# MLP second products as one level of Strassen's scheme: seven quarter-block products in place of eight

## The reference, cut to what matters

```
hm = rms_norm(x, g_mlp)                                 # x: 512 x 1024
x = x + square(relu(hm @ w_up)) @ w_down                # w_up: 1024 x 4096, w_down: 4096 x 1024
return rms_norm(x, g_final)
```

## Time and profile before

| what | us |
|---|---|
| median of 3 runs (1577.17 to 1579.16) | 1579.07 |
| the profiled execution | 1579.46 |
| its span, first to last instruction | 1577.7 |
| PE busy in the span | 1531.7 (97%) |
| DVE / ACT / POOL busy | 890.2 / 715.3 / 223.5 |
| granted TensorE clock, mean | 0.991 |

### The profile page before, as it was taken

The page is one execution under the profiler, slowest core; times in us unless marked ns, Lnnn a source line. Parts: engine busy times, 40 slices in busy tenths (PEclk is TensorE's granted clock), DMA queues, the critical chain, the costliest instruction groups (busy, mean ns, idle before and its releaser), DMA issues.

```text
span 1577.7 us, 19176 instructions
## 1 busy us (share of the span) xinstructions
PE 1531.7 (97%) x7086; PEld 1239.6 (79%) x7086; DVE 890.2 (56%) x1753; ACT 715.3 (45%) x1630; POOL 223.5 (14%) x194
## 2 busy tenths in 40 slices
PE   7998999999999999999899999999999999999998
PEld 5886777877898777777587878788777888888886
DVE  6467485657565566666457557664455444434344
ACT  6553343334355667665335354442344433324243
POOL 3203020202120003122022005220001100000001
PEclk9999999999999999999999999999999999999999
DMA  6522121323424221112133312134323333333332
GB/s 194 161 68 80 54 80 55 107 68 120 119 76 147 77 61 56 54 56 67 41 121 94 94 55 67 56 109 131 93 81 94 94 93 96 105 94 93 97 103 81
DMA packets 88636, 141.56 MB, mean 90 GB/s; under 512 B 6368, under 2 KB 36448, under 8 KB 88544
## 3 DMA queue, kind: packets, MB, share of 16 engines
q1 hardware_dynamic: 87824, 139.55, 29.3%
q10 hardware_dynamic: 720, 0.80, 0.2%
HBM read 138.23 MB, written 2.10 MB: 89 GB/s over the span
## 4 chain that ended last, share of the span: by engine, by line
PE 79%; DVE 8%; ACT 5%; issue 3%; POOL 3%; DMA 2%; SPq 0%; ACTq 0%; POOLq 0%; DVEq 0%
PE banks L1259 12%; PE banks L1261 12%; PE banks L1260 12%; PE banks L1264 10%; PE banks L1266 10%; PE banks L1265 10%; PE banks L1222 3%; DVE sb_w_split L1964 3%; ACT sb_junk L1529 2%; DVE sb_arena L1973 2%; PE banks L1437 1%; PE banks L1384 1%; ACT sb_w_split L1561 1%; PE banks L1500 1%; DVE sb_arena L1964 1%
## 5 line engine op out<-in xcount | busy, mean ns | idle before, releaser
L1964 DVE TENSOR_TENSOR sb_w_split<-sb_raw,sb_w_split 128x512 fp32r<-128x512 f32 (+4 forms) x530 | 345.0, 693 | 365.9 <-ACT sb_w_split L1561 365.5
L1561 ACT ACTIVATE sb_w_split<-sb_raw 128x512 fp32r<-128x512 f32 (+4 forms) x530 | 288.1, 592 | 411.2 <-PE banks L1261 192.0
L1259 PE MATMUL banks<-sb_actA,sb_w_split 128*128 128x512 f32 x672 | 277.1, 412 | 2.8 <-DVE sb_arena L1964 2.5
L1261 PE MATMUL banks<-sb_actA,sb_w_split 128*128 128x512 f32 x672 | 263.0, 391 | 0.0
L1260 PE MATMUL banks<-sb_actA,sb_w_split 128*128 128x512 f32 x672 | 262.1, 390 | 0.0
L1264 PE MATMUL banks<-sb_w_split,sb_actB 128*128 128x512 f32 (+2 forms) x464 | 181.4, 391 | 1.6 <-DVE sb_w_split L1964 1.6
L1266 PE MATMUL banks<-sb_w_split,sb_actB 128*128 128x512 f32 (+2 forms) x464 | 175.9, 379 | 0.0
L1265 PE MATMUL banks<-sb_w_split,sb_actB 128*128 128x512 f32 (+2 forms) x464 | 175.5, 378 | 0.0
L1264 PE MATMUL banks<-sb_w_split,sb_actA 128*128 128x512 f32 (+1 forms) x384 | 154.4, 402 | 13.5 <-DVE sb_w_split L1964 9.6
L1259 PEld LDWEIGHTS banks<-sb_actA,sb_w_split 128*128 128x128 f32 x672 | 126.5, 188 | 32.7 <-issue 7.1
L1266 PE MATMUL banks<-sb_w_split,sb_actA 128*128 128x512 f32 (+1 forms) x384 | 150.3, 391 | 0.0
(11 more groups left out here) (226 smaller groups left out, 2188.2 us busy)
## 6 DMA issues: line engine op xcount, KB each, us to landing
sb_raw<-in_a_w_in SPq DMA_DIRECT2D x66, 256.0 KB, 3.0
sb_raw<-in_w_up SPq DMA_DIRECT2D x32, 512.0 KB, 3.8
sb_raw<-in_w_down SPq DMA_DIRECT2D x32, 512.0 KB, 3.8
sb_raw<-in_w_in SPq DMA_DIRECT2D x24, 512.0 KB, 3.7
sb_raw<-in_mem_w_kv SPq DMA_DIRECT2D x16, 512.0 KB, 3.8
sb_raw<-in_w_ckv SPq DMA_DIRECT2D x16, 512.0 KB, 3.8
sb_raw<-in_a_w_in SPq DMA_DIRECT2D x15, 512.0 KB, 3.7
sb_raw<-in_a_w_out SPq DMA_DIRECT2D x12, 512.0 KB, 3.9
```

The lines of the kernel that those rows point to most:

```text
L1259: pe.op.matmul(out, hi[:, cs], x.hi(k), start=i == 0, stop=False)
L1261: t = pe.op.matmul(out, lo[:, cs], x.hi(k), start=False, stop=last_i)
L1561: act.op.activation(hi[:, cs], raw[:, cs], ACT.Copy).then_inc(act.mark(m("w_hi"), 2 * n + part + 1), 1)
L1964: dve.op.tensor_tensor(out, a, b, op).then_inc(dve.mark(*mark) if mark else dve.tick(), 1)
```

## The change

**The product.** Let a block's hidden activations be cut into quarters F(rows, cols), rows being two halves of the 512 tokens and cols two halves of the 1024 hidden units, and its block of `w_down` into quarters w0 to w3 of 512 x 512. Eight quarter products are replaced by seven: P1 = F00·w0, P2 = F01·w2, Q5 = S1·T1, P6 = S2·T2, Q3 = S4·w3, Q7 = S3·T3, N4 = -F11·T4, with sums S of activation quarters and T of weight quarters. Each is 2 banks (256 tokens) x 4 k-tiles: 2 chunks of 12 matmuls. Their order is P1, P2, Q5, P6, Q3, Q7, N4.

**Weights.** The quarters are loaded whole (`fetchR`, 1 MB each; w0 and w1 into arena space, w2 and w3 into the space of `x_res`, for block 0 only after the last `xt`). POOL makes T1, T3, T2, T4 in place (`tsum`), 1024 columns an instruction, two per sum. The splits of these chunks are one instruction of 1024 columns on ACT and one on DVE, not two of 512.

**Activations.** `relu` now evicts with the row of 1/r (a step `nrow` e on PE and ACT replaces `esum`), ACT squares into a plain buffer, and for each product and k-pair a step `g` (ACT high part, DVE low part) or `gp` (ACT high part, POOL low part) writes the operands. The sums are `s1` (DVE) and `ssum` 2, 4, 3 (POOL).

**Landing.** A product is added into `x_tok` and/or a buffer `first_sum`: ten landings, each over two token tiles, so 20 DVE instructions of 512 columns per block in place of 8 evictions. In block 3 six more POOL additions (`fix`) take `first_sum` over.

```diff
-            add(f"up{b}{g}", ("w_up",), D_MODEL, [(b * D_MODEL + g * 512, 512)], "feature", "hE", "relu")
-        for half in range(2):
-            add(f"dn{b}{half}", ("w_down",), D_MODEL, [(half * 512, 512)], "token", f"f{b}", "tok", k0=b * D_MODEL)
+            add(f"up{b}{g}", ("w_up",), D_MODEL, [(b * D_MODEL + g * 256 + c, 256) for c in (0, 512)], "feature", "hE", "relu")
+        for i in range(7):
+            add(f"wn{b}{i}", None, 512, [(0, 512)], "token", f"F{b}{i}", "wn" if len(LANDS[i]) == 1 else "wn2",
+                tokens=SEQ // 2)
...
+LANDS = {P1: (("x", 0, 0, ALU.add), ("sum", 0, 0, ALU.subtract)), P2: (("x", 0, 0, ALU.add),),
+         Q5: (("x", 0, 1, ALU.add), ("x", 1, 1, ALU.add)), P6: (("sum", 0, 0, ALU.add),), Q3: (("x", 0, 1, ALU.add),),
+         Q7: (("x", 1, 1, ALU.add), ("x", 1, 0, ALU.subtract)), N4: (("x", 1, 0, ALU.subtract),)}
...
+        if b:
+            p.soon.extend([[("fetchR", b, 0)], [("fetchR", b, 1)], [("tsum", b, 1, 0)], [("fetchR", b, 3)],
+                           [("tsum", b, 1, 1)], [("fetchR", b, 2)], [("tsum", b, 3, 0)], [("tsum", b, 3, 1)]])
...
+        p.soon.extend([[("g", b, P1, 0)], [("g", b, P2, 0)], [("s1", b, 0), ("g", b, Q5, 0)], [("ssum", b, 2, 0)],
+                       [("gp", b, P6, 0)], [("ssum", b, 4, 0)], [("gp", b, Q3, 0)], [("ssum", b, 3, 0)]])
+        p.product(f"up{b}1", into=banks(4) if b else (0, 1, 2, 3),
+                  tail=lambda j: [("relu", b, up_tile(1, j))] + ([("g", b, P1, 1)] if j == 1 else []))
+        if b == 0:
+            p.need(("tsum", 0, 3, 1))
+        work = {P1: [[("g", b, P2, 1)], [("s1", b, 1), ("g", b, Q5, 1)], [("gp", b, Q7, 0)], [("ssum", b, 2, 1)]],
+                P2: [[("tsum", b, 2, 0)], [("gp", b, P6, 1)], [("g", b, N4, 0)], [("tsum", b, 2, 1)]],
+                Q5: [[("ssum", b, 4, 1)], [("gp", b, Q3, 1)], [("ssum", b, 3, 1)], [("gp", b, Q7, 1)]],
+                P6: [[("g", b, N4, 1)], [("tsum", b, 4, 0)], [("tsum", b, 4, 1)]],
+                Q3: [[("fix", n)] for n in range(3)] if b == 3 else [], Q7: [], N4: []}
+        for i in WINO_ORDER:
+            p.soon.extend(work[i])
...
+            p.product(f"wn{b}{i}", into=banks(2), tail=tail, whole=b == 3 and i == N4)
```

In the split of such a chunk (ACT, then DVE), and in the sums on POOL:

```diff
+                made = {Q5: 1, P6: 2, Q7: 3, N4: 4}.get(i)
+                if made:
+                    act.wait_ge(*m.at("t_sum", ("tsum", b, made, c)))
+                else:
+                    act.wait_ge(m(f"dma_quarter{WEIGHT[i]}"), 16 * (b + 1))
+                act.wait_ge(*m.chunk_done(n - SPLIT_SLOTS))
+                act.op.activation(hi, raw, ACT.Copy).then_inc(act.mark(m("w_hi"), 2 * n + 2), 2)
...
+            elif t == 2:
+                pool.wait_ge(*m.wino_split(b, Q5, c))
+                tensor(total, total, w[3], ALU.add, *m.at("t_sum", step))
```

More of the change, by code:

```diff
@@ L408, in need, with product @@
                 self.force(step)
-    def product(self, name, before_ev=(), soon=None, into=None, first=True, tail=None):
+    def product(self, name, before_ev=(), soon=None, into=None, first=True, tail=None, whole=False):
         pr = PRODUCTS[name]
@@ L415, in product @@
         ks, i, n_j = k_tiles(name), 0, n_out(name)
-        spans = [(c,) for c in range(len(pr.order))] if tail is None else [(0,), tuple(range(1, len(pr.order)))]
+        spans = [tuple(range(len(pr.order)))] if whole else [(c,) for c in range(len(pr.order))]
         for span in spans:
@@ L778, in order_of_work @@
     p.put(("load_g",))
-    p.side(0, [("sqp", "e", 7)], lag=0)
-    p.side(0, (), ("nsq", "e"), ("esum",), lag=4000)
+    scales(0, "e", after=[("sqp", "e", 7)])
     for j in range(TT):
@@ L783, in order_of_work @@
             p.side(0, (), ("xt", j, g))
-    for b in range(4):
[L785 to L789, removed]
+    for i in (0, 1):
+        p.put(("fetchR", 0, i))
+    for i in (3, 2):
+        p.side(0, (), ("fetchR", 0, i))
@@ new lines, in order_of_work, with banks @@
+    for t in (1, 3):
+        for c in range(2):
+            p.side(0, (), ("tsum", 0, t, c), lag=0)
+    bank = 4
+    def banks(n):
+        nonlocal bank
+        bank = (bank + n) % 8
+        return [(bank - n + i) % 8 for i in range(n)]
+    for b in range(4):
+        if b:
+            p.soon.extend([[("fetchR", b, 0)], [("fetchR", b, 1)], [("tsum", b, 1, 0)], [("fetchR", b, 3)],
+                           [("tsum", b, 1, 1)], [("fetchR", b, 2)], [("tsum", b, 3, 0)], [("tsum", b, 3, 1)]])
+        p.product(f"up{b}0", [("nrow", "e")], into=banks(4) if b else (0, 1, 2, 3),
+                  tail=lambda j: [("relu", b, up_tile(0, j))])
+        p.soon.extend([[("g", b, P1, 0)], [("g", b, P2, 0)], [("s1", b, 0), ("g", b, Q5, 0)], [("ssum", b, 2, 0)],
[11 more added lines that the diff above has]
+            p.soon.extend(work[i])
+            tail = None
+            if b == 3 and i in (P2, Q7):
+                tail = lambda j: [("fsq", int(i == Q7), 2 * (i == Q7) + j), ("fg", 2 * (i == Q7) + j)]
+            elif b == 3 and i in (Q3, N4):
+                tail = lambda j: [(kind, *([int(i == Q3)] if kind == "fsq" else []), 2 * (i == N4) + j)
+                                  for kind in ("fsq", "fin", "store")]
+            p.product(f"wn{b}{i}", into=banks(2), tail=tail, whole=b == 3 and i == N4)
@@ L1174, in raw_total, with wino_split @@
     def raw_total(self, n):
-        return 16 * sum(len(PRODUCTS[self.plan.chunks[m][0]].parts) for m in range(n % RAW_SLOTS, n + 1, RAW_SLOTS))
+        return 16 * sum(len(PRODUCTS[self.plan.chunks[m][0]].parts) for m in range(n % RAW_SLOTS, n + 1, RAW_SLOTS)
+                        if not is_wino(self.plan.chunks[m][0]))
+    def wino_split(self, b, i, c):
+        return self("w_lo"), 2 * self.plan.chunk_of[f"wn{b}{i}", c] + 2
 class Stream:
```

225 lines of the change are left out of this document (181 added, 44 removed).

## The result

| | before | after |
|---|---|---|
| median, us | 1578.12 (1575.03 to 1579.16, 4 runs) | 1630.23 (1628.19 to 1634.11, 4 runs) |
| span of the profiled execution, us | 1577.7 | 1626.1 |
| granted TensorE clock, mean | 0.991 | 0.983 |

The ratio is 1.0344, 95% interval 1.0324 to 1.0364. The direction was forecast, the size was not: 52 us slower where I had 18, and outside the range of 1562 to 1612.

A forecast was written before the change was run, and what follows sets the result against it. PE bounds the kernel, busy 97% of the span. -21.8 + 0.4 + 4 x 8 (lateness) + 4 (block 0) + 3.5 (block 3 and end) = +18.1 on 1579.5 gives 1597.6, median 1597; range 1562 to 1612.

The forecast's parts named there:

- block 0: In block 0, w2 and w3 load late, so P2's first chunk is 4 us late beyond the usual lateness; bounds 0 to 6.
- block 3 and the end: In block 3, `fg` costs 2.2 us, Q3's chains ahead of N4's splits about 1, the end 0.6: together 3.5, from 0.6 to 6.
- PE's part: Down products: 96 matmuls fewer save 21.8 us, `nrow` adds 0.4; a block's seven products take 38.1 us, not 43.5.
- the prices of ACT and DVE: Seven products: ACT 1.05 us a 1024-column split, 0.63 a conversion; DVE 1.15 to 1.22 a split, 0.60 a landing.
- what costs nothing: Blocks 1 to 3, up products: loading the quarters and making T1 and T3 there adds no time.
- POOL's prices: POOL's sums: 2.0 us for 1024 columns, 1.05 for 512, making 15.4 us of work in the first four products.
- The turns: Seven products: DVE's splits, `g` and `s1` wait while a POOL addition runs, landings don't; without this the sum is 1578.
- case 1: The forecast: DVE, held by POOL, makes the first four products late, 6 to 10 us a block: 1588 to 1608; chance 0.50.
- case 4: POOL becomes the bound, ACT behind it: 13 us a block or more, stretches above 50 us, 1618; chance 0.10.
- Case 2: The turns don't matter, POOL falls into DVE's landings: 3.1 us a block, 1578, from 1573 to 1587; chance 0.14.
- case 3: Split slots hide nearly all lateness, PE stays the bound: 0 to 1.5 us a block, 1564, 1559 to 1572; chance 0.26.
- The walk: One block's seven products followed chunk by chunk: lateness 10 us with turns, 3.1 without; 8 taken, for turns possibly won.

The follow-up runs named there:

- pool_few: Changed kernel with GpSimd's weight sums, activation sums and low parts worked on 16 columns only, results left out: 1578.16 us, ratio 1.0008.
- pool_fill: Changed kernel with each of GpSimd's sums and low parts replaced by two memsets of its output, which read nothing from SBUF: 1585.06 us, ratio 1.0054.
- t4_late: Changed kernel with the two halves of weight sum T4 moved from P6's steps to Q3's in the list: 1623.84 us, ratio 1.029.
- late_fin: Changed kernel with block 3's `fg` of tiles 0 and 1 moved after Q3, their norm chains and stores after Q7's evictions: 1621.56 us, ratio 1.0285.
- close_on_vector: Kernel of on_vector's moves in the order just in time, with block 3's six repairs on VectorE too, the first one place later: 1589.2 us, ratio 1.0073.
- on_vector: Changed kernel with the sums and low parts that GpSimd makes inside the seven products moved to VectorE, same order: 1612.75 us, ratio 1.0224.
- the order just in time: on_vector's moves against the changed kernel, with sums placed near their use, copies of x earlier, block 3's closing work behind Q3 and Q7: 1590.31 us, ratio 1.0081.

## Why the prediction fell short

By the starts of the matmuls in the two profiled executions (before: stretches of 43.52 each):

| term | forecast | measured |
|---|---|---|
| 96 matmuls fewer | -21.8 | -21.8 |
| `nrow` | +0.4 | +0.5 |
| blocks 1 and 2 | 2 x 8 | 2 x 13.35 |
| block 0 | 8 + 4 | 18.4 |
| block 3 and the end | 8 + 3.5 | 26.2 + 0.3 |
| start of the up products (1218.1, 1216.2) | 0 | -2.0 |
| sum | +18.1 | +48.3, of 48.4 between the spans (rounding) |

Of the 30.2 us between the two sums, 21.4 are the four blocks' 13.35 for 8, 9.7 are block 3 and the end beyond that (13.2 for 3.5), 1.0 is block 0 (5.0 for 4) and 0.1 `nrow`; the start takes 2.0 off. Two terms failed, then: the lateness of a block, and the end. The row of the start is not the change's: in the profiled executions of all kernels the up products begin between 1211.6 and 1218.5.

**PE's part, the prices of ACT and DVE, and what costs nothing** held: splits 1.22 and landings 0.68 listed, ACT's 1.05, up products 43.52 with all quarters loaded and T1 and T3 made in them. POOL's prices did not hold: where nothing holds it, it lists 2.40 us for 1024 columns and 1.28 for 512, where I had 2.0 and 1.05, so its work in the four products was 18.6 us and not 15.4. Two slips of the working weigh little: DVE has six small instructions and not five (31.7 us, not 31), and 2 MB are four loads of 512 KB, not three, so block 0's low bound was taken for a shorter transfer.

**The turns** are shown by pool_few and pool_fill: the mechanism of case 1, and of case 4 (below). Case 2 is out (landings free, yet 13.35 us), and so is case 3.

**The walk** named the right chunks: 1.0, 0.8, 2.8, 1.3, 1.2 and 2.9 us late, measured 1.2, 0.6, 0.8 + 2.1, 1.5, 1.4 and 3.3. Its 10 became 10.9. The step that failed is the one after it: "a turn won there is worth 1 us; I take 8". No turn was won. The lateness is a sum of waits in series, and I had discounted its largest terms for luck. With 2.9 us a block that is some 12 of the 21.4 us. Most of the other 2.45 a block is the clock.

**The clock** was missing from the sum. PE in block 1, around a gap, and the granted clock of the two slow spells:

```profile
1386.35 0.47 PE L1370 MATMUL banks<-sb_w_split,sb_actB 128*128 128x512 f32 x1 [1.97 <-issue]
...
1387.58 0.43 PE L1372 MATMUL banks<-sb_w_split,sb_actB 128*128 128x512 f32 x1
1387.82 0.63 PE L1370 MATMUL banks<-sb_w_split,sb_actB 128*128 128x512 f32 x1
1388.24 0.63 PE L1371 MATMUL banks<-sb_w_split,sb_actB 128*128 128x512 f32 x1
```

```profile
1387.80:1391.20 3.40, 3.33 (x8) 2.15 (x7) 2.09 (x3) 1.21 (x2) 3.06 (x2) 0.50 0.00 0
1401.00:1404.40 3.40, 3.38 (x9) 2.67 (x10) 3.40 (x5) 0.00 (x0) 0.00 (x0) 0.57 0.02 5
```

The starts of matmuls are 0.43 us apart there, not 0.227: the lower level, 1.2 GHz. It came after idle times of 2.1 and 3.3 us and lasted some 3.4 us each time. In the MLP of the kernel before no matmul is so spaced. What it costs is less than what it slows: block 2, with the same gaps, has the second spell alone (8 starts 0.43 apart against 13) and the same 51.45 us. The first spell only fills time in which PE waits in block 2: the fifth and sixth gaps are 1.9 us together in block 1, and 2.8 in block 2. And t4_late has the same seven gaps in both blocks, but in its block 1 no such spell at all. Its blocks 1 and 2:

```profile
1363.67:1413.56 49.89, 40.10 (x170) 30.98 (x168) 41.15 (x43) 20.16 (x27) 25.80 (x13) 1.00 0.08 25
1457.08:1508.57 51.49, 41.67 (x169) 32.13 (x168) 41.40 (x43) 20.16 (x27) 25.83 (x13) 0.97 0.08 25
```

So the clock is worth 1.6 us of a steady block's 13.35. The rest of the 2.45 is mostly the second start after a gap, 0.31 to 0.34 us behind the first and not 0.227, together 0.6. In block 3, 25 starts are slow, by 4.9 us in all.

**Block 0**: 5.0 above the steady blocks, 4 forecast. Both reasons are in the timelines: ACT waits for the quarter, then T3's sums stand in the way of P2's low part.

```profile
1268.71 1.06 ACT L1671 ACTIVATE sb_w_split<-sb_x_res 128x1024 fp32r<-128x1024 f32 x1 [1.53 <-DMA sb_x_res<-in_w_down]
...
1271.11 6.14 POOL L2631 TENSOR_TENSOR sb_arena<-sb_arena,sb_x_res 128x1024 f32<-128x1024 f32 x2
...
1272.17 2.88 DVE L2085 TENSOR_TENSOR sb_actB<-sb_arena,sb_actB 128x512 fp32r<-128x512 f32 x1
```

The transfers were in time 5.5 us earlier than I had (1268.7, not 1274.2), and the sums cost what that saved.

**Block 3 and the end** is the term furthest off for its size: 12.9 us in the stretch beyond the steady blocks, and 0.3 at the end, against 3.5. I had priced the chains of Q3's tiles at 1 us on DVE, and had overlooked that each waits for a root on POOL, which stands behind six repairs. POOL, then ACT, then PE:

```profile
1594.76 9.47 POOL L2631 TENSOR_TENSOR sb_arena<-sb_arena 128x512 f32<-128x512 f32 x6 [1.76 <-DVE sb_arena L2085]
1604.19 0.56 POOL L2639 TENSOR_TENSOR sb_small<-sb_small,sb_cons 128x1 f32<-128x1 f32 x1
...
1604.84 0.72 ACT L1733 ACTIVATE sb_arena<-sb_arena,sb_small 128x512 f32<-128x512 f32 x1 [4.12 <-POOL sb_small L2639]
1608.63 1.99 ACT L1671 ACTIVATE sb_w_split<-sb_arena 128x1024 fp32r<-128x1024 f32 x2
...
1611.10 0.76 PE L1370 MATMUL banks<-sb_w_split,sb_arena_r 128*128 128x512 f32 x1 [8.18 <-issue]
```

N4's split follows the chains in ACT's list, and starts at 1608.63; PE has stood for 8.2 us. late_fin, which moves the chains and `fg`, brings the stretch to 51.8: shown for the two together, and for the chains by the gap of 8.3 us that is gone. pool_few keeps a gap of 7.7 there, so it is not GpSimd's sums but the six repairs and the order. The steps failed are thus "the chains of Q3's tiles stand on DVE ahead of N4's splits, about 1 us past what PE can wait" and the 2.2 us for `fg`: with it the gap before Q3's second chunk came 3.3 us later than in a steady block (35.8 us into the stretch, not 32.5).

**Case 4** gave 13 us a block and stretches above 50, and 13.35 and 51.45 came, so by my own sign the trace speaks for it. Over the whole stretch POOL is busy only 25.8 of 51.5 us, but where the products run late it is nearly always busy, and both of the case's reasons are in the trace: a sum of 1024 columns keeps the turn 2.2 us and is itself held (2.80 us listed on average), and ACT stands behind POOL. A window over the four products' middle, then one gap:

```profile
1374.00:1401.00 27.00, 19.56 (x72) 13.98 (x73) 23.07 (x20) 10.06 (x13) 23.11 (x11) 0.94 0.00 0
```

```profile
1385.13 2.27 POOL L2631 TENSOR_TENSOR sb_arena<-sb_arena 128x512 f32<-128x512 f32 x1
1387.43 0.63 ACT L2029 ACTIVATE sb_actB<-sb_arena 128x512 fp32r<-128x512 f32 x1 [6.13 <-POOL sb_arena L2631]
1389.11 1.39 DVE L2140 TENSOR_TENSOR sb_w_split<-sb_arena,sb_w_split 128x1024 fp32r<-128x1024 f32 x1 [2.86 <-ACT sb_w_split L1671]
```

PE waits for this split, VectorE was idle before it, and what had held it all up is GpSimd's queue. My walk had this wait too (behind `ssum` 4), as one of six. Cases 1 and 4 are one queue of turns seen from its two sides: pool_fill shows that without turns neither engine makes much lateness, and no run parts them further. Part of the fit is luck, since 1.6 us of the 13.35 are the clock, which the case did not have, and its 1618 missed by block 3.

Open: how far the closing order could still be improved (behind close_on_vector's last matmul two tiles' chains stand in series on DVE), and a last block made with the old eight products, which was not tried. With the best steady stretch found, 42.3 against 43.5, either way would win 1.2 us a block, under 5 us in all; whether another order comes nearer to the 38.1 of the matmuls is open too.

## What to carry to other kernels

Matmuls saved are worth only what the operand work leaves of them: here 5.4 us of TensorE a block were bought with 14.2 us of VectorE (32.9 in pool_few's stretch, where nothing holds it, against 18.7) and 25.8 of GpSimd, waits included, with 15.4 more of GpSimd in the up products. Before sums go to an idle GpSimd, ask whether they read SBUF while VectorE combines two SBUF inputs; if so they take VectorE's time as well, and longer than VectorE itself would need. When a walk with a hand-made schedule gives a number, take that number, allow for the clock after long gaps, and follow every small wait at the end (a root, a mean) to the queue that it stands in.

## What the runs showed of the hardware that I had not expected

- **The turn is dearer than the work.** VectorE needs 0.60 us for 512 columns and 1.14 for 1024; GpSimd's instruction holds it 1.1 and 2.2 us. Eleven such instructions a block moved to VectorE made the stretch 4.7 us shorter (on_vector), and 6.3 in the order just in time.
- **Memsets by GpSimd don't hold VectorE's splits**: one of 1024 columns is 1.22 us inside them.
- **TensorE's clock can fall in the middle of a busy stretch**: 3.4 us at half rate after idle times of 2.1 and 3.3 us, but not each time (the 2.1 us in block 2 had no such spell, nor had any gap in t4_late's block 1); in pool_few's steady stretches, with gaps of 1.2 and 0.6 us, no matmul is spaced so.
